# Recurrence chunks of a hybrid decoder layer: right-hand side's products before the inverse's first ones, GpSimd's first mask in two halves, bonus and decays behind the first additions

## The chip, the core and the metric

The kernel runs on one core of one Trainium2 chip. The metric is the device time of one execution in microseconds. Five engines work side by side and meet only through semaphores: TensorE (PE, with its weight loads shown apart as PEld), VectorE (DVE), ScalarE (ACT), GpSimd (POOL) and SyncE (SP), which issues DMAs.

## The reference, cut to what matters

One decoder layer over 1024 tokens of width 1024: an RWKV-7 recurrence of 8 heads x 64 beside differential attention, then cross-attention, then a top-4-of-32 expert network. The change touches the recurrence alone, which is

```python
def step(state, inp):
    r_t, w_t, k_t, v_t, kk_t, a_t = inp
    sa = jnp.einsum('bhvk,bhk->bhv', state, -kk_t)
    state = (state * w_t[:, :, None, :]
             + sa[..., None] * (kk_t * a_t)[:, :, None, :]
             + v_t[..., None] * k_t[:, :, None, :])
    return state, jnp.einsum('bhvk,bhk->bhv', state, r_t)
_, y = lax.scan(step, state0, scan_in)
```

with a bonus, `sum(r * k * r_k) * v` for each head, added to the result later. Everything is float32.

## The kernel before, in words

The recurrence (`rwkv_chunks`) is run in 8 chunks of 128 tokens. Within a chunk the step-by-step update is turned into products of 128x128 matrices for each of the 8 heads: the correlations of the tokens of the chunk (`corr`, four matrices for each head, masked by `corr_mask`), a triangular system whose inverse is wanted (`inv`, and transposed `invT`), a right-hand side (`rhs`), the solution, the new state and the output. The state couples one chunk to the next.

Each engine has its own list of instructions in the order in which the code of its block writes them, and each step adds one to the engine's semaphore; other engines wait for the value of a named step. So the order of the work is written out by hand. What one chunk does:

- **Start.** TensorE transposes `vc`, `kc` and `bc` into PSUM (L1134, step "turn"; ScalarE copies them to `vkb`, L1011) and makes the head sums for the bonus in `crossed` (L1136). VectorE makes `ar` (L1071, L1072) and scales the state (L1075).
- **Correlations and masks.** For each head TensorE writes 128x512 values into one of two PSUM banks (L1144, L1145), and VectorE multiplies them with the mask into `corr` (L1078). Two banks mean that TensorE is at most two heads ahead.
- **Level 0.** GpSimd multiplies the first matrix of every head with a level's mask into `part` (L989), 128x1024 values in one instruction. `part` has a single buffer. TensorE turns it over by a product with the identity into `straight` (L1152, two groups of four heads), VectorE adds the identity to `part` and to `straight` for `invT` and `inv` (L1095, L1097).
- **Right-hand side.** TensorE multiplies the state (L1158) and the correlations with the values (L1161) into `mixed`; ScalarE copies it to `rhs` (L1013), which is used only after the last level.
- **Levels 1 to 6** double the blocks of the inverse. In each, TensorE multiplies `part` with `inv` into `pairs` (L1170), ScalarE copies that (L1017), TensorE makes two further products (L1179, L1183), VectorE adds them into `inv` and `invT` (L1105, L1107), and GpSimd makes the next level's `part` (L989) meanwhile.
- **End.** TensorE solves (L1190), makes the new state and the output (L1196 to L1214); VectorE and ScalarE fold these in (L1114, L1118, L1022, L1025).

Beside this chain VectorE multiplies the bonus (L1082) and prepares the next chunk in parts: `prepare(i + 1, 0)` are the decays' differences (L1045, L1047, L1048, L1049), for which ScalarE takes exponentials after level 1's copies (L1001 to L1004); the further parts follow levels 1 to 3. GpSimd also copies `vc` once a chunk (L980).

One matmul of this float32 program stands as two records of the trace: the 8 products of L1152 are 16 records.

## Time and profile before

| | us |
|---|---|
| median of 3 runs | 3436.45 (3435.72 to 3442.59) |
| the profiled execution's own time | 3427.17 |
| its span | 3425.5 |
| busy in the span: PE, DVE, ACT, POOL | 2913.8, 1148.8, 669.2, 500.8 |
| mean granted TensorE clock | 0.922 |

The granted clock is TensorE's, as a share of full speed: 1.00 is 2.4 GHz and 0.50 is 1.2 GHz. The recurrence's 8 chunks lie between some 657 and 1130 us of the span, one after the other about every 60 us. The experts' products, from about 1760 us on, are the larger part of the kernel and are not touched.

### The profile page before, as it was taken

The numbers are of one execution on the slowest core, as the hardware profiler recorded it, in microseconds if no ns is written. First come the engines' busy times: TensorE is split into PE (matmuls) and PEld (weight loads), VectorE is DVE, ScalarE is ACT, GpSimd is POOL, SyncE is SP. The second block draws the span as 40 slices with busy tenths as digits, with TensorE's granted clock in tenths as the row PEclk, the third lists the DMA queues.
The fourth block names the chain that finished last, engine by engine and source line by source line (L and its number), as shares of the span: only waits on it lengthen the run. The fifth ranks groups of instructions, "written<-read, shape, count | busy, mean of one in ns | idle before, by whom it ended". The sixth has DMA issues, their size and how long they took to land. (4 is left out here: it accounts for less than half of the span.)

```text
span 3425.5 us, 54810 instructions
## 1 busy us (share of the span) xinstructions
PE 2913.8 (85%) x20974; PEld 2739.6 (80%) x20975; DVE 1148.8 (34%) x2439; ACT 669.2 (20%) x1261; POOL 500.8 (15%) x577
## 2 busy tenths in 40 slices
PE   7899888398999397986359999999999999999990
PEld 6876774288888396886359999999999999999990
DVE  2128221744443432232312222223222322232227
ACT  3139213111211312222001111111111111111111
POOL 0000001122213000001141110111111111111103
PEclk9999998699999698998579999999999999999995
DMA  6100210000000112014148877788888888888777
GB/s 223 32 25 1 56 43 7 0 1 0 0 0 0 51 55 69 12 56 151 53 135 298 286 269 270 270 292 294 291 292 293 288 297 286 292 294 276 270 260 260
DMA packets 320781, 543.61 MB, mean 159 GB/s; under 512 B 23584, under 2 KB 102176, under 8 KB 320672
## 3 DMA queue, kind: packets, MB, share of 16 engines
q1 hardware_dynamic: 301344, 499.67, 42.4%
q0 software_dynamic: 19360, 42.87, 4.1%
q8 instruction: 54, 0.88, 0.1%
q14 instruction: 23, 0.19, 0.0%
HBM read 506.01 MB, written 36.47 MB: 158 GB/s over the span
## 5 line engine op out<-in xcount | busy, mean ns | idle before, releaser
L2124 PE MATMUL experts_up<-experts_xs,g_pieces 128*128 128x144 f32 (+1 forms) x8192 | 1034.3, 290 | 114.4 <-DVE experts_xs L2053 77.4
L2124 PEld LDWEIGHTS experts_up<-experts_xs,g_pieces 128*128 128x128 f32 x8192 | 1027.7, 197 | 121.2 <-issue 121.2
L2147 PE MATMUL experts_down<-experts_hs,g_across 128*128 128x144 f32 (+1 forms) x3072 | 389.2, 289 | 0.0
L2147 PEld LDWEIGHTS experts_down<-experts_hs,g_across 128*128 128x128 f32 x3072 | 386.1, 190 | 0.0
L2002 POOL DMA_INDIRECT experts_x<-h_rows,experts_index x198 | 192.3, 971 | 1133.5 <-DVE experts_xs L2053 1078.6
L2083 DVE TENSOR_SCALAR experts_glu<-experts_up,experts_bias 128x176 f32<-128x176 f32 x256 | 102.3, 400 | 710.1 <-PE experts_up L2124 710.1
L2033 ACT ACTIVATE experts_sig<-experts_glu 128x352 f32<-128x352 f32 x128 | 63.7, 497 | 998.4 <-DVE experts_lin L2085 998.4
L2040 ACT ACTIVATE experts_yT<-experts_down,experts_bias 128x176 f32<-128x176 f32 x256 | 104.2, 407 | 381.1 <-PE experts_down L2147 305.8
L989 POOL TENSOR_TENSOR chunk_part<-chunk_corr,rwkv_level_mask 128x1024 f32<-128x1024 f32 x56 | 119.2, 2128 | 351.9 <-DVE chunk_corr L1078 188.5
L2074 DVE COPY experts_bias<-g_bias 128x24 f32 x32 | 5.8, 181 | 391.7 <-ACT experts_yT L2040 391.6
L2136 PE MATMUL experts_down<-experts_hs,g_across 128*128 128x144 f32 (+1 forms) x1024 | 133.3, 289 | 0.0
L2136 PEld LDWEIGHTS experts_down<-experts_hs,g_across 128*128 128x128 f32 x1024 | 130.1, 190 | 0.0
L1183 PE MATMUL chunk_crossed<-chunk_invT,chunk_corr 128*128 128x64 f32 x768 | 100.4, 275 | 0.0
L2085 DVE TENSOR_SCALAR experts_lin<-experts_up,experts_bias 128x176 f32<-128x176 f32 x256 | 100.4, 392 | 0.0
L1170 PE MATMUL chunk_pairs<-chunk_inv,chunk_part 128*128 128x128 f32 x768 | 96.4, 279 | 1.4 <-POOL chunk_part L989 1.4
L1183 PEld LDWEIGHTS chunk_crossed<-chunk_invT,chunk_corr 128*128 128x128 f32 x768 | 92.8, 192 | 0.3
L1170 PEld LDWEIGHTS chunk_pairs<-chunk_inv,chunk_part 128*128 128x128 f32 x768 | 89.6, 192 | 2.0 <-issue 1.8
L1017 ACT COPY chunk_corr<-chunk_pairs 128x512 f32<-128x512 f32 x96 | 56.2, 585 | 168.0 <-PE chunk_pairs L1170 168.0
L1105 DVE TENSOR_TENSOR chunk_inv<-chunk_inv,chunk_straight 128x256 f32<-128x256 f32 x80 | 33.7, 422 | 163.7 <-PE chunk_crossed L1183 163.7
L1481 PE MATMUL w_out_product<-w_out_w_high,hc_high 128*128 128x256 f32 x256 | 73.9, 289 | 16.2 <-DVE w_out_w_low L1413 16.2
L1179 PE MATMUL chunk_straight<-chunk_corr,chunk_invT 128*128 128x64 f32 x640 | 86.1, 277 | 0.0
L2053 DVE STREAM_TRANSPOSE experts_xs<-experts_x 128x256 f32<-128x256 f32 x198 | 68.3, 408 | 52.2 <-DMA experts_x<-h_rows,experts_index 52.2
(377 smaller groups left out, 4408.1 us busy)
## 6 DMA issues: line engine op xcount, KB each, us to landing
g_pieces<-in_w_dram SPq DMA_DIRECT2D x132, 2048.0 KB, 8.1
g_across<-in_w_dram SPq DMA_DIRECT2D x64, 2048.0 KB, 9.3
y_rows<-experts_y SPq DMA_DIRECT2D x132, 192.0 KB, 3.9
g_across<-in_w_ckv_dram SPq DMA_DIRECT2D x8, 1024.0 KB, 10.2
rkv_raw<-in_w_in_dram SPq DMA_DIRECT2D x13, 512.0 KB, 3.9
diff_qk_raw<-in_w_in_dram SPq DMA_DIRECT2D x9, 512.0 KB, 4.0
cross_q_raw<-in_w_cq_dram SPq DMA_DIRECT2D x9, 512.0 KB, 4.3
m_u<-in_x_dram SPq DMA_DIRECT2D x8, 512.0 KB, 10.1
```

Of the source, the lines that this page charges most:

```text
L989: pool.tensor_tensor(part[:], corr[:, :, 0, :], level_mask[:, l, :].unsqueeze(1).to_broadcast([P, H, P]), ALU.mult).then_inc(*pool_steps.s ...
L1170: ins = pe.matmul(pairs[:, g, j * P:(j + 1) * P], part[:, h, :], inv[:, h, :], start=(j == 0), stop=(j == 3), skip_group_check=True)
L1179: pe.matmul(level(straight, g, l)[:, j], invT[:, h, :], half(prod[:, h:h + 1, :], l, 0)[:, 0], start=(j == 0), stop=(j == 3), skip_group_c ...
L1183: ins = pe.matmul(level(crossed, g, l)[:, j], prod[:, h, :], half(invT[:, h:h + 1, :], l, 1)[:, 0], start=(j == 0), stop=(j == 3), skip_gr ...
L1481: pe.matmul(to, high[:, k, now], w_high[:, c % 2, k, :], start=(k == 0), stop=False)
L2002: pool.indirect_dma_start(x[:, g, :], None, quarters, bass.IndirectOffsetOnAxis(ap=index[:, 1, g:g + 1], axis=0)).then_inc(x_in, 16)
L2040: act.activation(yT[:, n, 0:N], down[:, n % 4, 0:N], ACT.Identity, bias=bias[:, 16 + n:17 + n]).then_inc(*act_y.step(f"d{n}"))
L2083: dve.tensor_scalar(glu[:, s, j, :], up[:, u % 4, 0:N], bias[:, 2 * u:2 * u + 1], LIMIT, ALU.add, ALU.min).then_inc(*dve_hidden.step(f"glu ...
L2085: dve.tensor_scalar(lin[:, s, j, :], up[:, u % 4, N:2 * N], bias[:, 2 * u + 1:2 * u + 2], 1.0 - LIMIT, ALU.add, ALU.max).then_inc(*dve_hid ...
L2124: ins = pe.matmul(up[:, u % 4, l * N:l * N + w], raw[c][:, k, at:at + 255:2], xs[:, k, 0:w], start=(k == 0), stop=(k == 7), skip_group_che ...
L2136: ins = pe.matmul(down[:, n, 0:w], raw[4][:, k, n * P:(n + 1) * P], hs[:, k, 0:w], start=(k == 0), stop=(k == 7), skip_group_check=True)
L2147: ins = pe.matmul(down[:, n % 4, 0:w], raw[4 + n // 4][:, k, (n % 4) * P:(n % 4 + 1) * P], hs[:, k, 0:w], start=(k == 0), stop=(k == 7), s ...
```

## The change

Four things, all in `rwkv_chunks`:

1. TensorE makes the right-hand side's products directly behind the correlations, after a new wait for the last head's mask, and the level-0 products after them. Before, level 0 came first.
2. GpSimd makes level 0's `part` in two instructions of four heads each. The first needs only the first four heads' masks, and TensorE waits for each half by itself.
3. VectorE does the four additions of level 0 directly behind the masks, and the bonus and `prepare(i + 1, 0)` behind them.
4. TensorE waits for the bonus before level 1's second products, since those write the PSUM bank from which the bonus is read.

The names of the steps are put in the new order. No arithmetic is added; GpSimd has one instruction more in each chunk.

```diff
--- before.py
+++ after.py
@@ -932,12 +932,12 @@
         groups = range(2)
         level_names = [f"l{l}_{what}{g}" for l in range(1, LEVELS) for what in ("p", "q") for g in groups]
         pe_steps = S.steps("products", ["turn", "bonus"] + [f"corr{h}" for h in range(H)] +
-                           ["l0_0", "l0_1", "rhs"] + level_names + ["solve", "state", "y"])
+                           ["rhs", "l0_0", "l0_1"] + level_names + ["solve", "state", "y"])
         act_steps = S.steps("act", ["v", "k", "b", "rhs"] +
                             [f"l{l}_p{g}" for l in range(1, LEVELS) for g in groups] + ["solve", "y"])
-        pool_steps = S.steps("pool", ["v"] + [f"part{l}" for l in range(LEVELS)])
-        dve_steps = S.steps("vector", ["r", "a", "edge", "state_in"] + [f"mask{h}" for h in range(H)] + ["bonus"] +
-                            [f"l0_{w}{g}" for g in groups for w in ("t", "s")] +
+        pool_steps = S.steps("pool", ["v", "part0_0", "part0_1"] + [f"part{l}" for l in range(1, LEVELS)])
+        dve_steps = S.steps("vector", ["r", "a", "edge", "state_in"] + [f"mask{h}" for h in range(H)] +
+                            [f"l0_{w}{g}" for g in groups for w in ("t", "s")] + ["bonus"] +
                             [f"l{l}_{w}{g}" for l in range(1, LEVELS) for g in groups for w in ("s", "t")
                              if not (l == LEVELS - 1 and w == "s")] +
                             ["add0", "add1", "scale0", "scale1"])
@@ -978,13 +978,16 @@
                     pool.wait_ge(pe_steps.sem, pe_steps.value("turn", i - 1))
                     pool.wait_ge(pool_steps.sem, pool_steps.so_far(i))
                     pool.tensor_copy(vc[:], u[:, 8:12, now]).then_inc(*pool_steps.step("v"))
-                    pool.wait_ge(dve_steps.sem, dve_steps.value(f"mask{H - 1}", i))
-                    for l in range(LEVELS):
-                        if l >= 1:
-
-                            pool.wait_ge(pe_steps.sem, pe_steps.value("l0_1" if l == 1 else f"l{l - 1}_p1", i))
-                            if l == 1:
-                                pool.wait_ge(dve_steps.sem, dve_steps.value("l0_s1", i))
+                    for g in groups:
+                        pool.wait_ge(dve_steps.sem, dve_steps.value(f"mask{4 * g + 3}", i))
+                        pool.tensor_tensor(
+                            part[:, 4 * g:4 * g + 4], corr[:, 4 * g:4 * g + 4, 0, :],
+                            level_mask[:, 0, :].unsqueeze(1).to_broadcast([P, 4, P]), ALU.mult).then_inc(*pool_steps.step(f"part0_{g}"))
+                    for l in range(1, LEVELS):
+
+                        pool.wait_ge(pe_steps.sem, pe_steps.value("l0_1" if l == 1 else f"l{l - 1}_p1", i))
+                        if l == 1:
+                            pool.wait_ge(dve_steps.sem, dve_steps.value("l0_s1", i))
                         pool.wait_ge(pool_steps.sem, pool_steps.so_far(i))
                         pool.tensor_tensor(
                             part[:], corr[:, :, 0, :],
@@ -1077,24 +1080,24 @@
                         dve.wait_ge(pe_steps.sem, pe_steps.value(f"corr{h}", i))
                         dve.tensor_tensor(corr[:, h], pairs[:, h % 2, :].rearrange("p (c n) -> p c n", n=P),
                                           corr_mask[:], ALU.mult).then_inc(*dve_steps.step(f"mask{h}"))
+                    eye = C.ident[:].unsqueeze(1).to_broadcast([P, 4, P])
+
+                    def four(x, g):
+                        return x[:, g * 4:g * 4 + 4, :]
+
+                    def bank(x, g):
+                        return x[:, g, :].rearrange("p (h n) -> p h n", n=P)
+                    for g in groups:
+                        dve.wait_ge(pool_steps.sem, pool_steps.value(f"part0_{g}", i))
+                        dve.tensor_tensor(four(invT, g), four(part[:], g), eye, ALU.add).then_inc(*dve_steps.step(f"l0_t{g}"))
+                        dve.wait_ge(pe_steps.sem, pe_steps.value(f"l0_{g}", i))
+                        dve.tensor_tensor(four(inv, g), bank(straight, g), eye, ALU.add).then_inc(*dve_steps.step(f"l0_s{g}"))
                     dve.wait_ge(pe_steps.sem, pe_steps.value("bonus", i))
 
                     dve.tensor_tensor(r, crossed[:, 1, :].rearrange("p (c n) -> p c n", n=P), vc[:],
                                       ALU.mult).then_inc(*dve_steps.step("bonus"))
                     if more:
                         prepare(i + 1, 0)
-                    eye = C.ident[:].unsqueeze(1).to_broadcast([P, 4, P])
-
-                    def four(x, g):
-                        return x[:, g * 4:g * 4 + 4, :]
-
-                    def bank(x, g):
-                        return x[:, g, :].rearrange("p (h n) -> p h n", n=P)
-                    dve.wait_ge(pool_steps.sem, pool_steps.value("part0", i))
-                    for g in groups:
-                        dve.tensor_tensor(four(invT, g), four(part[:], g), eye, ALU.add).then_inc(*dve_steps.step(f"l0_t{g}"))
-                        dve.wait_ge(pe_steps.sem, pe_steps.value(f"l0_{g}", i))
-                        dve.tensor_tensor(four(inv, g), bank(straight, g), eye, ALU.add).then_inc(*dve_steps.step(f"l0_s{g}"))
                     for l in range(1, LEVELS):
                         for g in groups:
                             dve.wait_ge(pe_steps.sem, pe_steps.value(f"l{l}_q{g}", i))
@@ -1146,13 +1149,7 @@
                                   skip_group_check=True).then_inc(*pe_steps.step(f"corr{h}"))
 
                     pe.wait_ge(act_steps.sem, act_steps.value("b", i))
-                    pe.wait_ge(pool_steps.sem, pool_steps.value("part0", i))
-                    for g in groups:
-                        for j in range(4):
-                            ins = pe.matmul(straight[:, g, j * P:(j + 1) * P], part[:, g * 4 + j, :], C.ident[:],
-                                            start=(j == 0), stop=(j == 3), skip_group_check=True)
-                        ins.then_inc(*pe_steps.step(f"l0_{g}"))
-
+                    pe.wait_ge(dve_steps.sem, dve_steps.value(f"mask{H - 1}", i))
                     pe.wait_ge(act_steps.sem, act_steps.value("y", i - 1))
                     for c in range(CT):
                         pe.matmul(mixed[:, 0, c * P:(c + 1) * P], ar[:, c, 0, :], state[:, c, :], start=(c == 0),
@@ -1161,6 +1158,13 @@
                         ins = pe.matmul(mixed[:, 0, h * 64:(h + 1) * 64], corr[:, h, 2, :], vkb[:, 0, h * 64:(h + 1) * 64],
                                         start=False, stop=(h == H - 1), skip_group_check=True)
                     ins.then_inc(*pe_steps.step("rhs"))
+                    for g in groups:
+                        pe.wait_ge(pool_steps.sem, pool_steps.value(f"part0_{g}", i))
+                        for j in range(4):
+                            ins = pe.matmul(straight[:, g, j * P:(j + 1) * P], part[:, g * 4 + j, :], C.ident[:],
+                                            start=(j == 0), stop=(j == 3), skip_group_check=True)
+                        ins.then_inc(*pe_steps.step(f"l0_{g}"))
+
                     for l in range(1, LEVELS):
                         pe.wait_ge(pool_steps.sem, pool_steps.value(f"part{l}", i))
                         for g in groups:
@@ -1170,6 +1174,8 @@
                                 ins = pe.matmul(pairs[:, g, j * P:(j + 1) * P], part[:, h, :], inv[:, h, :],
                                                 start=(j == 0), stop=(j == 3), skip_group_check=True)
                             ins.then_inc(*pe_steps.step(f"l{l}_p{g}"))
+                        if l == 1:
+                            pe.wait_ge(dve_steps.sem, dve_steps.value("bonus", i))
                         for g in groups:
                             pe.wait_ge(act_steps.sem, act_steps.value(f"l{l}_p{g}", i))
                             pe.wait_ge(dve_steps.sem, dve_steps.value(f"l{l - 1}_t{g}", i))
```

TensorE in a chunk, between the last head's correlations and level 1, before (a row is an instruction or a run of equal ones: what is written, what is read, and x the count; REGISTER_ALU and ISA rows only prepare waits):

```order
L1145 MATMUL chunk_pairs<-chunk_ar,chunk_kc 128x256
L1148 ISA
L1149 REGISTER_ALU
L1152 MATMUL chunk_straight<-g_ident,chunk_part 128x128 x8
L1156 ISA
L1158 MATMUL chunk_mixed<-chunk_state,chunk_ar 128x128 x4
L1161 MATMUL chunk_mixed<-chunk_vkb,chunk_corr 128x64 x8
L1165 REGISTER_ALU
L1167 REGISTER_ALU
L1170 MATMUL chunk_pairs<-chunk_inv,chunk_part 128x128 x4
L1167 REGISTER_ALU
L1170 MATMUL chunk_pairs<-chunk_inv,chunk_part 128x128 x4
```

And in the changed kernel, the same stretch:

```order
L1148 MATMUL chunk_pairs<-chunk_ar,chunk_kc 128x256
L1151 ISA
L1152 REGISTER_ALU
L1153 ISA
L1155 MATMUL chunk_mixed<-chunk_state,chunk_ar 128x128 x4
L1158 MATMUL chunk_mixed<-chunk_vkb,chunk_corr 128x64 x8
L1162 REGISTER_ALU
L1164 MATMUL chunk_straight<-g_ident,chunk_part 128x128 x4
L1162 REGISTER_ALU
L1164 MATMUL chunk_straight<-g_ident,chunk_part 128x128 x4
L1169 REGISTER_ALU
L1171 REGISTER_ALU
L1174 MATMUL chunk_pairs<-chunk_inv,chunk_part 128x128 x4
```

The products for `mixed` have moved ahead of those for `straight`, and each group of four heads has its own wait.

VectorE in a chunk from the last mask to the first additions of level 0, before:

```order
L1082 TENSOR_TENSOR m_u<-chunk_crossed,chunk_vc 128x4x128
L1044 ISA
L1045 ISA
L1045 TENSOR_TENSOR chunk_early<-rwkv_fall 128x512
L1046 REGISTER_ALU
L1047 REGISTER_ALU
L1047 TENSOR_TENSOR chunk_early<-chunk_early,rwkv_sig 128x512
L1048 COPY chunk_next_edge<-chunk_early 128x4
L1049 COPY chunk_next_edge<-rwkv_fall 128x4
L1093 ISA
L1095 TENSOR_TENSOR chunk_invT<-chunk_part,g_ident 128x512
L1096 REGISTER_ALU
```

And in the changed kernel from the last mask on:

```order
L1091 ISA
L1092 TENSOR_TENSOR chunk_invT<-chunk_part,g_ident 128x512
L1093 REGISTER_ALU
L1094 TENSOR_TENSOR chunk_inv<-chunk_straight,g_ident 128x512
L1091 REGISTER_ALU
L1092 TENSOR_TENSOR chunk_invT<-chunk_part,g_ident 128x512
L1093 REGISTER_ALU
L1094 TENSOR_TENSOR chunk_inv<-chunk_straight,g_ident 128x512
L1095 REGISTER_ALU
L1097 TENSOR_TENSOR m_u<-chunk_crossed,chunk_vc 128x4x128
L1047 ISA
L1048 ISA
```

The bonus (`m_u<-chunk_crossed,chunk_vc`) and the decays' differences (`chunk_early`, `chunk_next_edge`), which stood between the masks and the additions, now follow the additions.

## Rows read from the trace of the kernel before

**Rows 1.** The page, part 2: granted TensorE clock, tenths of full speed, 40 slices.
```profile
PEclk9999998699999698998579999999999999999995
```

**Rows 2.** Who waited for whom, 658 to 1128 us: us in total, times, longest.
```profile
POOL chunk_part L989 <- DVE chunk_corr L1078: 188.5, 8, 23.9
...
PE chunk_straight L1152 <- POOL chunk_part L989: 24.5, 8, 3.1
```

**Rows 3.** Timeline of one chunk, masks to level 1: start us, us, engine, line.
```profile
726.30 0.59 PE L1145 MATMUL chunk_pairs<-chunk_ar,chunk_kc 64*128 64x256 f32 x2
726.33 1.29 DVE L1078 TENSOR_TENSOR chunk_corr<-chunk_pairs,rwkv_corr_mask 128x512 f32<-128x512 f32 x2 [0.62 <-PE chunk_pairs L1145]
...
727.78 2.12 POOL L989 TENSOR_TENSOR chunk_part<-chunk_corr,rwkv_level_mask 128x1024 f32<-128x1024 f32 x1 [23.86 <-DVE chunk_corr L1078]
728.14 2.31 DVE L1045 TENSOR_TENSOR chunk_early<-rwkv_fall 128x512 f32 x1
...
729.96 3.63 PE L1152 MATMUL chunk_straight<-g_ident,chunk_part 128*128 128x128 f32 x16 [3.06 <-POOL chunk_part L989]
...
732.07 0.69 DVE L1097 TENSOR_TENSOR chunk_inv<-chunk_straight,g_ident 128x512 f32<-128x512 f32 x1
732.67 0.68 DVE L1095 TENSOR_TENSOR chunk_invT<-chunk_part,g_ident 128x512 f32<-128x512 f32 x1
...
733.42 1.06 PE L1158 MATMUL chunk_mixed<-chunk_state,chunk_ar 128*128 128x128 f32 x8
733.62 0.69 DVE L1097 TENSOR_TENSOR chunk_inv<-chunk_straight,g_ident 128x512 f32<-128x512 f32 x1 [0.27 <-PE chunk_straight L1152]
...
734.31 1.90 PE L1161 MATMUL chunk_mixed<-chunk_vkb,chunk_corr 128*128 128x64 f32 x16
734.47 2.12 POOL L989 TENSOR_TENSOR chunk_part<-chunk_corr,rwkv_level_mask 128x1024 f32<-128x1024 f32 x1 [4.57 <-DVE chunk_inv L1097]
...
736.72 2.05 PE L1170 MATMUL chunk_pairs<-chunk_inv,chunk_part 128*128 128x128 f32 x16 [0.51 <-POOL chunk_part L989]
...
738.63 1.10 PE L1179 MATMUL chunk_straight<-chunk_corr,chunk_invT 128*128 128x64 f32 x8
```

**Rows 4.** PE in two other chunks: the one quickest and the one slowest there.
```profile
846.14 0.59 PE L1145 MATMUL chunk_pairs<-chunk_ar,chunk_kc 64*128 64x256 f32 x2
849.80 3.45 PE L1152 MATMUL chunk_straight<-g_ident,chunk_part 128*128 128x128 f32 x16 [3.06 <-POOL chunk_part L989]
...
856.39 2.05 PE L1170 MATMUL chunk_pairs<-chunk_inv,chunk_part 128*128 128x128 f32 x16 [0.51 <-POOL chunk_part L989]
...
965.81 0.59 PE L1145 MATMUL chunk_pairs<-chunk_ar,chunk_kc 64*128 64x256 f32 x2
969.47 3.78 PE L1152 MATMUL chunk_straight<-g_ident,chunk_part 128*128 128x128 f32 x16 [3.06 <-POOL chunk_part L989]
973.04 1.92 PE L1158 MATMUL chunk_mixed<-chunk_state,chunk_ar 128*128 128x128 f32 x8
974.75 2.33 PE L1161 MATMUL chunk_mixed<-chunk_vkb,chunk_corr 128*128 128x64 f32 x16
976.91 2.00 PE L1170 MATMUL chunk_pairs<-chunk_inv,chunk_part 128*128 128x128 f32 x16
```

**Rows 5.** Stretches, PE alone: us, busy and records, granted clock, DMA.
```profile
661.60:665.00 3.40, 3.40 (x12) 0.50 0.00 0
...
671.80:675.20 3.40, 3.40 (x18) 0.50 0.00 0
...
726.90:729.90 3.00, 0.00 (x0) 1.00 0.00 0
729.90:733.30 3.40, 3.35 (x15) 0.50 0.00 0
...
736.70:767.20 30.50, 30.48 (x267) 1.00 0.00 0
...
968.80:975.60 6.80, 6.13 (x29) 0.50 0.00 0
```

## The prediction

> **What bounds the kernel now.** I read the page's line of granted clocks first [rows 1]: a slice is 85.6 us, the recurrence begins in the eighth, which reads 6, and fills the next five, which read 9, so the clock varies there and has to be looked at closer. The list of waits in that stretch [rows 2] shows one thing that TensorE waits for in all 8 chunks: GpSimd's first `part`, 24.5 us in 8 times, 3.1 at the longest. GpSimd in turn waits for the last mask, but that is idle time of an engine with little to do.
>
> The timeline of one chunk [rows 3] gives the chain around it. The last mask ends at 726.33 + 1.29 = 727.62. GpSimd starts at 727.78 and takes 2.12. TensorE, idle since it ended the correlations, starts level 0 (L1152) at 729.96; the row says that it was idle for 3.06. VectorE's last addition starts at 733.62, within 0.03 of the modelled end of L1152, and ends at 734.31. GpSimd starts level 1's `part` at 734.47 (one buffer, so not earlier), takes 2.12 again, and L1170 starts at 736.72. The right-hand side's products (733.42 to 736.21) run in the shadow of that second `part`. From L1170 on TensorE bounds the chunk: in 30.5 us of levels it is busy for 30.48 [rows 5], so whatever comes earlier or slower there moves the end one for one.
>
> The stretches [rows 5] show what the idle 3.06 us bring with them. The clock is 1.00 up to 729.9 and 0.50 in the 3.4 us behind, which is 1.2 instead of 2.4 GHz. L1152's 16 records take 3.63 us, where 16 records of the same 128x128 form take 2.05 in L1170 at full clock [rows 3]. In two other chunks L1152 takes 3.45 and 3.78, and in the second the half clock reaches over L1158 (1.92 instead of 1.06) and L1161 (2.33 instead of 1.90) [rows 4]. So every chunk has one long idle of TensorE, one fall of the clock with it, and pays for it on the products behind.
>
> From the start of the last L1145 row to L1170 the chunks of rows 3 and 4 take 10.42, 10.25 and 11.10 us. 10.25 and 11.10 are the least and the most of the seven chunks that follow the first one; their mean, read in the same way, is 10.58.
>
> **The changed chain.** All at full clock, on the times of rows 3:
> - Right-hand side first: it starts behind the last mask, at 727.62 + 0.06 (what L1152 needs after GpSimd: 727.78 + 2.12 to 729.96) = 727.68. It takes 736.21 - 733.42 = 2.79. It ends at 730.47.
> - GpSimd's halves: no row has this instruction on 512 values a partition. It takes at least half of 2.12, or 1.06, and at most the whole 2.12. The second half starts at 727.78 and ends at 728.84 to 729.90; the first is done during the masks. Either value is before 730.47, so the price is nothing. I take 1.1.
> - Level 0: 16 records need 738.63 - 736.72 = 1.91 as L1170 shows. First group issued by 731.43, second by 732.38; the ends are 0.14 later (2.05 - 1.91).
> - Additions: the first (`part` plus identity) is made during the right-hand side. It meets GpSimd's second half, and a row shows what that can do: L1045, 2.31 us under GpSimd's instruction, where VectorE's neighbours of the same size take 0.69. Even with all of 1.6 more it ends by 730, before it is needed. Then three more, 0.60 apart (732.07 to 732.67): 731.60, 732.20, 732.80, and 0.69 for the last: 733.49.
> - GpSimd: 0.16 later, 2.12 long: 735.77. TensorE 0.13 behind it (736.59 to 736.72): 735.90.
>
> From 726.30 that is 9.60 instead of 10.58: **0.98 us less in a chunk, 7.8 us in eight**.
>
> What moved behind the additions is covered. The bonus (0.69) starts at 733.40 and ends near 734.1, before TensorE begins level 1, so its new wait costs nothing. The decays' differences take 2.31 for L1045, 0.69 for another of the usual size and two copies of 8 values or less, to about 737.3. ScalarE wants them when it has copied level 1's first products, which are not made before 735.90 + 2.05 = 737.95; VectorE's next additions follow the second products, which start 1.91 behind L1170 and take 1.10 for the first part, so after 738.9. The cover is 0.6 us at least; if it were gone, ScalarE's exponentials would be late by the rest, and their reader comes a level later. ScalarE's copy `rhs` comes earlier and is used at the end of the chunk. No DMA or queue is touched.
>
> **Where the clock goes.** The change does not take away the idle time, it moves it. TensorE's idle before level 0 shrinks from 3.06 to about 0.8 (726.9 to 727.68). But nothing is left to do behind level 0: from 732.52 to 735.90, for 3.38 us, TensorE waits for the additions and the second `part`. In all 8 chunks an idle of 3.06 to 3.08 was followed by a half clock at once. A longer one should be too, and the products that then pay are level 1's, with no cover behind them. I price that from the same rows: what L1152, L1158 and L1161 took beyond 2.05, 1.06 and 1.90. In rows 3 this is 1.58, in rows 4 it is 1.40 and 1.73 + 0.86 + 0.43 = 3.02, and over the seven chunks the mean is 2.15. So the sum is -0.98 + 2.15 = +1.17 us a chunk, **+9.4 us in eight**. With 1.40 and 3.02 for it, the two ends are +3.4 and +16.3.
>
> The old chain also paid this, but part of it in the shadow of GpSimd: in rows 3 L1158 and L1161 could have been slower by 0.5 at no cost.
>
> The Trainium skill has a rule that speaks against this change, in "TensorE: Matmul & The Clock Gate", section "HAM oscillation — how this bites in real kernels": a burst of products behind a long wait starts with a throttled clock, every time anew, and costs half of the throttled time. Applied to half-clock stretches of 3.4 and 6.8 us, the page's half would be 1.7 and 3.4 a chunk, an estimate of +6 to +19 us in eight. This trace agrees on the mechanism: 1.58 lost in a stretch of 3.4.
>
> **The rivals.**
> - **The clock holds, 0.13.** If TensorE's work in front (4.7 us without a pause, where before there were correlations with pauses) keeps the granted clock at 1.00 across the idle 3.38 and over L1170, only the gain is left: -7.8 us. It decides at one place, the clock over the first L1170 of each chunk. Against it stand 8 falls in 8 chunks after 3.06 us.
> - **A mixed case, 0.25.** The fall comes in some chunks, or comes early and lies mostly in the idle time, so that a chunk loses 0.4 to 1.4. In the chunk of rows 4 at 965.81 the clock was already at half from 968.8, and 0.7 us of that stretch were idle. Sum: 8 x (-0.98 + 0.4 to 1.4), -4.6 to +3.4. That the change's reordering does nothing to the time belongs here.
> - **The half clock lasts, 0.14.** At the first chunk it held from 661.6 to 675.2, 13.6 us, although TensorE was busy for all 3.4 us of its first and of its last part [rows 5]: being busy is not enough to get the clock back. Two thirds of a level's records are 128x64 products, narrower than L1152's. If the clock stays at half for 10 us of levels, a chunk loses 5: +4.0 a chunk. In half of the chunks, the others as forecast, +21 us; in all of them +32.
> - **The half clock comes under the right-hand side, 0.05.** The idle before it is short, but the correlations have pauses too. Its 24 records at L1152's 3.63 / 16 = 0.227 take 5.4 instead of 2.8, and level 0 would take 3.6 instead of 1.9: +4.3 on the path, +26 us in eight with the gain.
>
> **How the numbers follow.** The forecast has the rest, 0.43. On the profiled execution it is 3427.17 + 9.4 = 3436.6. That execution is 9.3 below the median of the three runs; the difference is carried over unchanged: 3436.45 + 9.4 = 3445.8. The forecast's own range is 3439.9 to 3452.8. The range that should hold 8 in 10 takes in most of the mixed case below and the partly long half clock above: 3431 to 3458. A difference of 0.2%, 6.9 us, is about what a measurement of this kernel can tell from none. Faster by more: the clock holds, 0.13. Slower by more: three quarters of the forecast, 0.32, with the two last rivals, 0.19: 0.51. Within it: 0.36.
>
> **What would show it.** Right: L1174 (now level 1's first product) starts about 9.6 us after the last L1148 row instead of 10.6; TensorE's long idle stands before it, 3.4 us, released by GpSimd, and that before level 0 is gone; level 0 takes 1.9 to 2.1 us; the granted clock is 0.50 behind the idle, and one or two levels of each chunk take 7 us or more instead of 48 records x 30.48 / 267 = 5.48. GpSimd's halves take 1.1 us. Wrong: a clock of 1.00 over level 1 in most chunks, or a half clock under the right-hand side, or level 1's copies or second products that wait for VectorE.

## The result

| | us |
|---|---|
| before, median of 4 runs | 3436.52 (3435.72 to 3442.59) |
| changed, median of 4 runs | 3456.39 (3453.54 to 3458.44) |
| ratio of changed to before, with 95% interval | 1.0053 (1.0036 to 1.0071) |
| profiled execution before | 3427.17, span 3425.5 |
| profiled execution of the changed kernel | 3455.29, span 3453.7 |

The changed kernel is slower by 19.9 us. The forecast was +9.4, with a range of 3431 to 3458: the sign and the range held, and the forecast was half of what came.

### The profile page after: what moved, and what is told of

It is laid out like the page before. It is cut to its first block and busy times, and to the rows that moved or that the text cites. A ratio compares the mean times of both kernels' runs of the same rounds, so it can differ in the third digit from the quotient of the medians.

```text
span 3453.7 us, 54838 instructions
## 1 busy us (share of the span) xinstructions
PE 2934.1 (85%) x20974; PEld 2751.9 (80%) x20975; DVE 1148.7 (33%) x2439; ACT 664.6 (19%) x1261; POOL 505.4 (15%) x585
## 5 line engine op out<-in xcount | busy, mean ns | idle before, releaser
L1174 PE MATMUL chunk_pairs<-chunk_inv,chunk_part 128*128 128x128 f32 x768 | 106.5, 297 | 26.5 <-POOL chunk_part L992 26.5
L992 POOL TENSOR_TENSOR chunk_part<-chunk_corr,rwkv_level_mask 128x1024 f32<-128x1024 f32 x48 | 102.2, 2129 | 182.7 <-PE chunk_pairs L1174 136.9
L1174 PEld LDWEIGHTS chunk_pairs<-chunk_inv,chunk_part 128*128 128x128 f32 x768 | 99.1, 209 | 28.0 <-issue 24.5
L1487 PE MATMUL w_co_product<-w_co_w_high,w_co_high 128*128 128x256 f32 x256 | 73.9, 289 | 13.4 <-DVE w_co_w_low L1419 13.4
## 6 DMA issues: line engine op xcount, KB each, us to landing
g_across<-in_w_ckv_dram SPq DMA_DIRECT2D x8, 1024.0 KB, 10.1
m_u<-in_x_dram SPq DMA_DIRECT2D x8, 512.0 KB, 10.3
```

Of the source, the lines that this page charges most:

```text
L992: pool.tensor_tensor(part[:], corr[:, :, 0, :], level_mask[:, l, :].unsqueeze(1).to_broadcast([P, H, P]), ALU.mult).then_inc(*pool_steps.s ...
L1174: ins = pe.matmul(pairs[:, g, j * P:(j + 1) * P], part[:, h, :], inv[:, h, :], start=(j == 0), stop=(j == 3), skip_group_check=True)
L1487: pe.matmul(to, high[:, k, now], w_high[:, c % 2, k, :], start=(k == 0), stop=False)
```

## The profile after

First the changed kernel's line of granted clocks (the page, part 2), which answers to [rows 1]. The recurrence now lies at 655 to 1144 us.

```profile
PEclk9999998798998698998579999999999999999995
```

The eighth slice reads 7 instead of 6, but the tenth and the thirteenth read 8 instead of 9. Inside the recurrence something costs clock that did not before. The list of waits of the same stretch, 655 to 1130 us (us in all, times, longest), answers to [rows 2]:

```profile
POOL chunk_part L983 <- DVE chunk_corr L1081: 181.0, 16, 20.0
...
POOL chunk_part L992 <- DVE chunk_inv L1094: 45.9, 8, 7.9
...
PE chunk_pairs L1174 <- POOL chunk_part L992: 26.5, 8, 3.4
```

TensorE's wait of 24.5 us in 8 times before level 0 has become one of 26.5 us in 8 times before level 1. It has moved, and it is longer. The timeline of a quiet chunk, one whose clock falls only at level 1 (start, us, engine, line), for [rows 3]:

```profile
722.16 0.59 PE L1148 MATMUL chunk_pairs<-chunk_ar,chunk_kc 64*128 64x256 f32 x2
723.63 1.15 PE L1155 MATMUL chunk_mixed<-chunk_state,chunk_ar 128*128 128x128 f32 x8 [0.88 <-DVE chunk_corr L1081]
724.62 1.90 PE L1158 MATMUL chunk_mixed<-chunk_vkb,chunk_corr 128*128 128x64 f32 x16
726.35 2.00 PE L1164 MATMUL chunk_straight<-g_ident,chunk_part 128*128 128x128 f32 x16
731.80 3.14 PE L1174 MATMUL chunk_pairs<-chunk_inv,chunk_part 128*128 128x128 f32 x16 [3.44 <-POOL chunk_part L992]
734.73 1.59 PE L1185 MATMUL chunk_straight<-chunk_corr,chunk_invT 128*128 128x64 f32 x8
736.16 1.05 PE L1189 MATMUL chunk_crossed<-chunk_invT,chunk_corr 128*128 128x64 f32 x8
```

From the last correlation row to level 1 it is 731.80 - 722.16 = 9.64 us, where the prediction had 9.60. Level 0 takes 2.00, at full clock. TensorE then sits idle for 3.44 us, and level 1's first products take 3.14 instead of 2.05. The same stretch on the other engines, in the first chunk:

```profile
661.77 1.29 DVE L1081 TENSOR_TENSOR chunk_corr<-chunk_pairs,rwkv_corr_mask 128x512 f32<-128x512 f32 x2 [0.62 <-PE chunk_pairs L1148]
662.98 0.68 DVE L1092 TENSOR_TENSOR chunk_invT<-chunk_part,g_ident 128x512 f32<-128x512 f32 x1
663.14 1.53 POOL L983 TENSOR_TENSOR chunk_part<-chunk_corr,rwkv_level_mask 128x512 f32<-128x512 f32 x1 [2.67 <-DVE chunk_corr L1081]
...
668.28 0.68 DVE L1094 TENSOR_TENSOR chunk_inv<-chunk_straight,g_ident 128x512 f32<-128x512 f32 x1
668.88 0.68 DVE L1097 TENSOR_TENSOR m_u<-chunk_crossed,chunk_vc 128x512 f32 x1
669.13 2.12 POOL L992 TENSOR_TENSOR chunk_part<-chunk_corr,rwkv_level_mask 128x1024 f32<-128x1024 f32 x1 [4.45 <-DVE chunk_inv L1094]
...
671.38 3.53 PE L1174 MATMUL chunk_pairs<-chunk_inv,chunk_part 128*128 128x128 f32 x16 [3.44 <-POOL chunk_part L992]
```

The order of events is the one worked out: last addition, second `part`, level 1. Nothing waits for the bonus, which is done 1.8 us before level 1 starts.

So the quiet chunk explains little of 20 us. The third chunk shows where the rest is (TensorE only):

```profile
783.40 0.63 PE L1148 MATMUL chunk_pairs<-chunk_ar,chunk_kc 64*128 64x256 f32 x1
783.73 0.63 PE L1147 MATMUL chunk_pairs<-chunk_ar,chunk_bc 64*128 64x256 f32 x1
784.16 1.05 PE L1148 MATMUL chunk_pairs<-chunk_ar,chunk_kc 64*128 64x256 f32 x2
786.09 2.07 PE L1155 MATMUL chunk_mixed<-chunk_state,chunk_ar 128*128 128x128 f32 x8 [0.88 <-DVE chunk_corr L1081]
787.96 3.51 PE L1158 MATMUL chunk_mixed<-chunk_vkb,chunk_corr 128*128 128x64 f32 x16
791.26 3.30 PE L1164 MATMUL chunk_straight<-g_ident,chunk_part 128*128 128x128 f32 x16
797.70 3.51 PE L1174 MATMUL chunk_pairs<-chunk_inv,chunk_part 128*128 128x128 f32 x16 [3.14 <-POOL chunk_part L992]
```

The right-hand side takes 5.38 us instead of 2.89 and level 0 3.30 instead of 2.00, and the whole of the correlations takes 9.35 instead of 7.46. Two stretches of the same chunk (us, busy and records, granted clock, DMA):

```profile
780.40:794.00 13.60, 12.72 (x51) 0.50 0.00 0
797.40:800.80 3.40, 3.10 (x14) 0.50 0.00 0
```

The clock was at half from within the correlations to within level 0, 13.6 us, and fell once more behind the idle. Read out for every chunk from the two timelines, in us. The length runs from the first record of the `kc` correlations (L1145, now L1148) to that of the next chunk. "To level 1" starts at the last such record alone, not at the row of two that the timelines show, and so is 0.2 less. Level 1 runs to level 2's first product.

| chunk | 1 | 2 | 3 | 4 | 5 | 6 | 7 | 8 |
|---|---|---|---|---|---|---|---|---|
| length, before | 62.3 | 59.8 | 60.0 | 59.7 | 60.0 | 60.5 | 59.6 | |
| length, changed | 60.4 | 60.6 | 65.7 | 60.6 | 65.7 | 60.6 | 65.6 | |
| to level 1, before | 10.8 | 10.2 | 10.4 | 10.0 | 10.4 | 10.9 | 10.1 | 10.6 |
| to level 1, changed | 9.4 | 9.4 | 13.1 | 9.4 | 13.1 | 9.4 | 13.1 | 9.3 |
| level 1, before | 5.5 | 5.5 | 5.5 | 5.5 | 5.5 | 5.5 | 5.5 | 5.4 |
| level 1, changed | 6.9 | 7.0 | 6.9 | 7.0 | 6.9 | 7.0 | 6.9 | 7.0 |

From that first record to the start of the last chunk's solution the recurrence grew from 470.4 to 488.0 us, by 17.6. The spans of the two profiled executions differ by 28.2 us in all. Of the rest 12.9 lie behind the recurrence, in code that the change does not touch, and -2.3 before it. That part varied in the runs below too, though no edit touches it (2295 to 2306 us in them, 2297 and 2310 in these two). The changed kernel's second profile (e10) has 2295 there. So it isn't explained by the change.

The first chunk was 2.4 us longer before than its next ones, and this isn't the change's doing either. TensorE, nearly idle, was at half clock ahead of the recurrence, in code that no edit touches, and in this execution the half clock reached 1.5 us into the chunk's correlations:

```profile
607.00:658.20 51.20, 6.00 (x22) 0.50 0.00 0
```

In the changed kernel that stretch ended at 654.0 us, ahead of the chunk. It reached into the first chunk also in e11, e3 and e8 below, with old and new code, and in none of the others.

## The experiments

Two theories. **Clock:** the change's added time is TensorE's half clock, behind the moved idle and in three chunks' correlations; GpSimd's halves and VectorE's new order are harmless or good. **Waits:** it is VectorE's late bonus and decays, and TensorE's new wait for them. Ratios are against the kernel before, run on the same chip, with 95% intervals; the recurrence is measured as above, on one profiled execution each. For e2 and e3 that was the slowest of their runs (3461.63 and 3439.95 us), for e4 and e8 the fastest (3429.04 and 3420.48), so these rows don't show a typical execution.

| run | median us | before there | ratio | recurrence us |
|---|---|---|---|---|
| level 0 first (e1) | 3410.34 | 3430.49 | 0.994 (0.9923 to 0.9957) | 450.6 |
| right-hand side first, alone (e2) | 3453.50 | 3430.49 | 1.0063 (1.0046 to 1.0079) | 494.5 |
| changed, idle filled (e3) | 3433.33 | 3430.49 | 1.0005 (0.9996 to 1.0015) | 480.9 |
| before, idle filled (e4) | 3433.71 | 3430.49 | 1.0011 (1.0001 to 1.002) | 474.2 |
| changed, correlations filled (e5) | 3454.34 | 3429.78 | 1.0064 (1.004 to 1.0088) | 495.5 |
| changed, both filled (e6) | 3426.48 | 3429.78 | 0.999 (0.998 to 1.0) | 461.3 |
| level 0 first, correlations filled (e7) | 3399.98 | 3429.78 | 0.9916 (0.99 to 0.9933) | 442.5 |
| halves alone (e8) | 3424.49 | 3429.78 | 0.9986 (0.9975 to 0.9996) | 467.3 |
| VectorE's order alone (e9) | 3427.63 | 3428.88 | 0.9995 (0.9983 to 1.0007) | 467.0 |

**e1: level 0 first again, the rest of the change kept.**

```diff
-                    pe.wait_ge(dve_steps.sem, dve_steps.value(f"mask{H - 1}", i))
+                    for g in groups:
+                        pe.wait_ge(pool_steps.sem, pool_steps.value(f"part0_{g}", i))
+                        for j in range(4):
+                            ins = pe.matmul(straight[:, g, j * P:(j + 1) * P], part[:, g * 4 + j, :], C.ident[:],
+                                            start=(j == 0), stop=(j == 3), skip_group_check=True)
+                        ins.then_inc(*pe_steps.step(f"l0_{g}"))
```

The same lines go away behind the right-hand side, and the names of the steps are put in the old order.

> The changed kernel with one part undone: TensorE makes level 0's products before the right-hand side's again, and GpSimd's two halves and VectorE's new order stay. Clock theory (the added time is the half clock, which TensorE's idle between level 0 and level 1 and the phase of the chunks bring; halves and new order are harmless or good): the right-hand side again lies under the second part of GpSimd, level 0 starts at once with the first half, no idle of 3 us is left, and from the last correlation row to level 1 it is about 7.0 us instead of 10.6 before and 9.4 changed. That is 3.6 us a chunk or 25 to 30 us in eight below the kernel before, with the clock at 1.00 in most levels. Wait theory (the added time is the later bonus and decays on VectorE and TensorE's new wait for the bonus): level 1 stays at 6.9 us or more in this kernel too, and it is 5 to 20 us slower than before.

It is 20 us faster than before: 0.6% below, where the changed kernel is 0.5% above. Undoing this one part turns the sign. The waits theory falls. In the timeline of a chunk:

```profile
723.86 0.59 PE L1148 MATMUL chunk_pairs<-chunk_ar,chunk_kc 64*128 64x256 f32 x2
...
724.38 1.16 PE L1155 MATMUL chunk_straight<-g_ident,chunk_part 128*128 128x128 f32 x8
...
726.84 1.16 PE L1155 MATMUL chunk_straight<-g_ident,chunk_part 128*128 128x128 f32 x8 [1.30 <-POOL chunk_part L983]
...
727.84 1.06 PE L1161 MATMUL chunk_mixed<-chunk_state,chunk_ar 128*128 128x128 f32 x8
...
731.15 2.05 PE L1173 MATMUL chunk_pairs<-chunk_inv,chunk_part 128*128 128x128 f32 x16 [0.52 <-POOL chunk_part L992]
```

The first group starts without an idle, the second behind one of 1.30, and the right-hand side fills the wait for the second `part`. From the correlation row to level 1 it is 7.29 us; 7.0 had been expected. The miss against 25 to 30 us is the clock again: the fifth and the seventh chunk had a half clock in their correlations and took 59.4 us instead of 56.7, and the first 60.0.

**e2: TensorE's order alone, on the kernel before.**

```diff
-                    pe.wait_ge(pool_steps.sem, pool_steps.value("part0", i))
-                    for g in groups:
...
+                    pe.wait_ge(dve_steps.sem, dve_steps.value(f"mask{H - 1}", i))
                     pe.wait_ge(act_steps.sem, act_steps.value("y", i - 1))
...
                     ins.then_inc(*pe_steps.step("rhs"))
+                    pe.wait_ge(pool_steps.sem, pool_steps.value("part0", i))
+                    for g in groups:
...
```

The wait for GpSimd and level 0's products move behind the right-hand side.

> The kernel before with TensorE's order alone changed (right-hand side first, behind a wait for the last mask); one GpSimd instruction for level 0 and VectorE's old order. Clock theory: as the changed kernel within 5 us, so +13 to +25 us against before: the second idle of 3.4 us and the half clock behind it are there, and the halves never mattered for it, since the right-hand side's products cover the whole instruction of GpSimd. Wait theory: within 5 us of the kernel before, or faster by up to 8 us.

As the clock theory had it, +0.63% where the changed kernel has +0.53%. The reordering on TensorE alone brings a loss of that size. Level 0 starts 3.98 us behind the last correlation record with GpSimd's single instruction as with the halves: under the right-hand side's cover the halves were worth nothing. The falls aren't the same ones, though. The clock fell in the correlations of the fourth and the seventh chunk and under the right-hand side of the second, and in the first and the last it stayed at half for 10 us or more over level 1, which took 10.3 and 9.3 us there.

**e3: the changed kernel with the idle filled.** 12 products behind level 0 go to a PSUM bank that nobody reads at that time; they add work to the kernel and no result.

```diff
+                    for _ in range(12):
+                        pe.matmul(mixed[:, 1, 0:P], C.ident[:], ar[:, 0, 1, :], start=True, stop=True, skip_group_check=True)
```

> The changed kernel with 12 products added behind level 0 whose result nobody reads, 24 records or 2.7 us at full clock, where TensorE else sits idle for 3.4 us. Clock theory: they keep the granted clock at 1.00 over level 1, which then takes 5.5 us instead of 6.9 to 7.0, a gain of 1.45 us a chunk or 12 us in eight; whether the three chunks with a half clock in their correlations keep it depends on where the chunks come to lie, so 12 to 28 us below the changed kernel. Wait theory: level 1 is as long as in the changed kernel, and the time the same or longer.

Level 1 takes 5.5 us in all eight chunks. So the half clock in level 1 does come from the idle before it. The median is 20 us below e2's on the same chip, that of the kernel before and not under it. In the profiled execution, the slowest of ten, the half clock still came in the correlations or the right-hand side of five chunks (60.7 to 64.6 us, and the last one), while the three undisturbed ones took 58.9 to 59.1.

**e4: the kernel before with its own idle filled**, by the same 12 products behind the correlations. TensorE's wait for ScalarE's last copy of `mixed`, whose bank they write, moves ahead of them; level 0 starts 3.45 us behind the last correlation record in the undisturbed chunks as before, so that wait costs nothing there.

> The kernel before with the same 12 products added behind the correlations, where TensorE is idle for 3.06 us. Clock theory: level 0 runs at full clock, 1.9 to 2.1 us instead of 3.45 to 3.79, and the stretch from the last correlation row to level 1 falls from 10.6 to about 9.0 us: 10 to 15 us faster than before. Wait theory has nothing against this, but if the time stays as it is, the half clock had never cost anything and my price for it in the changed kernel falls too.

The 10 to 15 us did not come: the kernel was 3.2 us slower. Level 0 does run at full clock,

```profile
843.34 2.94 PE L1151 MATMUL chunk_mixed<-chunk_ar,g_ident 128*128 128x128 f32 x24
846.48 2.05 PE L1155 MATMUL chunk_straight<-g_ident,chunk_part 128*128 128x128 f32 x16 [0.20 <-POOL chunk_part L989]
848.37 1.06 PE L1161 MATMUL chunk_mixed<-chunk_state,chunk_ar 128*128 128x128 f32 x8
849.26 1.90 PE L1164 MATMUL chunk_mixed<-chunk_vkb,chunk_corr 128*128 128x64 f32 x16
852.76 2.46 PE L1173 MATMUL chunk_pairs<-chunk_inv,chunk_part 128*128 128x128 f32 x12 [1.59 <-POOL chunk_part L989]
```

and the way to level 1 is 9.7 us instead of 10.4. But the right-hand side is done early now, 1.59 us of idle stand before level 1, and the clock falls elsewhere: in two chunks level 1 took 7.0, in four the correlations (from their first `kc` record to the last) took 8.0 to 8.2 instead of 6.55. A fall that is prevented in one place came in another. And where that happened, the added products ran at half clock too and held level 0 up, as in the sixth chunk:

```profile
967.33 5.49 PE L1151 MATMUL chunk_mixed<-chunk_ar,g_ident 128*128 128x128 f32 x24
972.61 2.02 PE L1155 MATMUL chunk_straight<-g_ident,chunk_part 128*128 128x128 f32 x16
```

Level 0 starts 5.84 us behind the last correlation record there instead of 3.45.

**e5: the changed kernel with the correlations' pauses filled**, by 2 products before the first correlation and 3 before the third.

```diff
+                    for _ in range(2):
+                        pe.matmul(mixed[:, 1, 0:P], C.ident[:], kc[:, 0, :], start=True, stop=True, skip_group_check=True)
                     pe.wait_ge(dve_steps.sem, dve_steps.value("state_in", i))
...
+                        if h == 2:
+                            for _ in range(3):
+                                pe.matmul(mixed[:, 1, 0:P], C.ident[:], kc[:, 0, :], start=True, stop=True, skip_group_check=True)
```

> The changed kernel with 5 products (10 records) added whose result nobody reads: 2 before the first correlation and 3 before the third, where TensorE is idle for 0.3 and 0.8 us. If the half clock in three chunks' correlations comes from these pauses in products of half height, it goes: all chunks take 60.6 us, the time falls by some 13 to 16 us against the changed kernel, and level 1 still takes 6.9 to 7.0 us. Rival: the fall there is a late effect of the one behind the long idle, or of when a chunk begins, and pauses don't matter; then some chunks still take about 65 us and the time stays within 5 us of the changed kernel.

The 13 to 16 us did not come, though what was filled was cured: every chunk's correlations took 6.57 us. The kernel was 24.6 us slower than before where the changed one is 19.9, and its recurrence was 7.5 us longer than the changed kernel's. In the fourth chunk (same columns as above):

```profile
842.10:848.90 6.80, 6.59 (x38) 1.00 0.00 0
848.90:852.20 3.30, 2.24 (x12) 1.00 0.00 0
852.20:859.10 6.90, 6.90 (x36) 0.51 0.00 0
859.10:862.50 3.40, 0.71 (x6) 1.00 0.00 0
862.50:866.00 3.50, 3.03 (x14) 0.51 0.00 0
```

The fall came later, behind the correlations' end with its idle of 0.88, and lay over the right-hand side and level 0; 3.4 us at full clock, mostly idle, followed, and then the next fall. This came in four chunks, and in three the half clock stayed over level 1 for 10.2 us or more, so that level 1 took 9.0 to 10.3 us. So the correlations' own pauses are a cause, but not the only one that has to go.

**e6: both fillings in the changed kernel.**

> The changed kernel with both kinds of added products, 5 among the correlations and 12 behind level 0. If all that the change added is the half clock, every chunk now takes about 59.1 us as the undisturbed ones of the run with 12 did, 0.9 less than before the change: 5 to 12 us faster than the kernel before, and 25 to 30 us faster than the changed one. Rival (something else in the change costs time): not faster than before.

Every chunk but the last takes 59.15 us. From 657 to 1090 us the clock holds:

```profile
657.00:1090.00 433.00, 413.18 (x3374) 1.00 0.00 0
```

The recurrence takes 461.3 us, 9.1 less than before (2.4 of them for the first chunk's slow start there) and 26.7 less than the changed kernel. In time it is 3.3 us faster than before, less than the 5 to 12 expected and with an interval that ends at 1.0; in the trace the recurrence's gain is plain. With the clock held the change's chain is worth what its first term said, and nothing else in it costs time. A timed pair with the changed kernel on one chip wasn't made; e5, on the same chip, was 27.9 us slower.

**e7: level 0 first, and the correlations filled.**

> The kernel with GpSimd's halves and VectorE's new order but level 0 first, with the 5 products among the correlations added. There two chunks of eight had a half clock in the correlations and took 2.7 us longer. If the pauses make it, all chunks take 56.7 us, or up to 0.3 more where the added products delay a correlation: 3 to 8 us faster than without them, 22 to 28 faster than the kernel before. Rival: no change within 3 us, or slower by what the added products take, 10 records or 1.1 us a chunk.

29.8 us faster than before, more than the 22 to 28 expected: 3399.98 against 3429.78, the best of this study. Every chunk takes 56.8 us, and again

```profile
657.00:1090.00 433.00, 411.74 (x3349) 1.00 0.00 0
```

The 10 added records cost 0.07 us a chunk against e1's quiet ones, and its two falls in the correlations are gone. The first chunk's is gone too; in e1 it came at 703.9 us, within the solution, and why it is absent here isn't shown.

**e8: GpSimd's halves alone** (VectorE's bonus and decays back before the additions, level 0 first).

> The kernel before with GpSimd's halves alone; VectorE does the bonus and the decays before the additions, as before. VectorE is then busy with them until 3.7 us after the last mask, so the additions end about when they did (0.5 us earlier), although level 0's products are made 2 to 3 us earlier. TensorE does the right-hand side early and then is idle for 3 us before level 1, with the half clock behind it: level 1 takes 6.5 to 7 us. Sum: -0.5 + 1.4 a chunk, 0 to +15 us against before. Rival: the halves carry the whole gain of the kernel with level 0 first, -15 to -25 us.

This missed both: it was 5.3 us faster, where 0 to 15 us slower had been expected and the rival had 15 to 25 faster. Level 1 starts 8.66 us behind the last correlation record instead of 10.4, so 1.7 earlier where 0.5 had been worked out. VectorE's first instruction for the decays is 1.0 of the difference: beside a GpSimd instruction of 1.16 us it took 1.27 instead of 2.31, and the additions began that much earlier.

```profile
725.48 1.16 POOL L982 TENSOR_TENSOR chunk_part<-chunk_corr,rwkv_level_mask 128x512 f32<-128x512 f32 x1 [2.67 <-DVE chunk_corr L1080]
725.91 1.27 DVE L1047 TENSOR_TENSOR chunk_early<-rwkv_fall 128x512 f32 x1
```

The half clock over level 1 came in four chunks only, though it lasted 10 us in two of them.

**e9: VectorE's new order alone.**

> The kernel before with VectorE's new order alone (additions, then bonus and decays, and TensorE's wait for the bonus); one GpSimd instruction for level 0 and level 0 first on TensorE. The additions wait for TensorE's level 0 in any case, which is at half clock behind the idle of 3.06 us, so the chunk's chain stays as it was: from the last correlation row to level 1 10.0 to 10.9 us, the sum within 5 us of the kernel before. That and the run with the halves alone would show that the gain of both together needs both. Wait theory, last form: the later bonus delays level 1's second products; then level 1 takes over 5.6 us at full clock and the time is 5 us or more above before.

As expected: 1.3 us faster, inside the noise; 10.0 to 10.6 us to level 1, and level 1 in 5.5. Halves and order are worth 3.3 us a chunk together on the way to level 1 (10.4 to 7.07) and 1.7 and 0.2 apart. Either one alone leaves the other engine last.

**The two kernels once more**, unaltered.

> The changed kernel once more, unaltered, for a second profile. If the falls in the correlations follow from when the chunks come and are steady, again 2 to 4 of the 8 chunks take about 65 us and the others 60.4 to 60.9; if they were chance, another count from 0 to 8.

> The kernel before once more, unaltered. If it keeps its clock in the correlations for a reason, again all chunks from the second on take 59.5 to 60.5 us; if that was luck in one execution, one or more take 62 us or longer.

Both repeat to 0.1 us in every chunk: the changed kernel has its 65.7 us in the third, fifth and seventh again and a recurrence of 488.0, the other 59.6 to 60.5 from the second on and 470.4. So the falls aren't the chance of one execution. One execution each took 3442.22 and 3426.13 us, 16.1 apart.

**Why three chunks and why these.** The traces of all the runs answer it. In each of the 13 profiled executions every change of the granted clock lies on one even raster of time, to 0.003 us. What counts is where a point of that raster lies in a chunk, measured from the chunk's first correlation record:

| chunks | raster point at 4.06 to 4.64 us | number | clock fell within the correlations |
|---|---|---|---|
| nothing added among the correlations | yes | 15 | in all 15, at that point |
| the same | no; the nearest at 4.03 and 4.78 | 61 | in none |
| products added there (e5, e6, e7) | yes | 6 | in none |
| the same | no | 18 | in none |

The four first chunks that began at half clock are left out. In all 76 chunks with nothing added, the correlation records of the first 4.06 us start at the same times behind the first, to 0.005 us. In the kernel before, no chunk from the second on has a raster point in that stretch; the seventh comes nearest, with 4.01. In the changed one the third, the fifth and the seventh have it at 4.43 to 4.46, in both profiles. There a long and a short chunk together, 126.3 us, are to 0.01 us a whole number of the raster's spacings, so every second chunk comes to lie at the same place. No run shifted the chunks and did nothing else; the rule rests on these 100 chunks as they came to lie.

## Why the prediction was right, and where its size failed

- **The chain, -0.98 us a chunk.** Right: 9.64 instead of 9.60 from correlation row to level 1, and 9.43 instead of a mean of 10.4 from the last record in quiet chunks, -0.94.
- **Prices set at nothing.** Right: the halves lie under the right-hand side, the bonus and the decays under level 1. e6 has all of them and is faster in the recurrence. The second half took 1.53 us, between the two bounds; 1.1 had been taken.
- **The moved idle and the half clock behind it.** The mechanism was right in 8 chunks of 8: an idle of 3.44 (3.38 worked out) and level 1 at half clock, which e3 takes away. Its size was too large: 2.15 was taken from the old chunks, 6.95 - 5.5 = 1.45 came. In the old chunks the half clock lasted 3.4 us in three, at a cost of 1.40 to 1.67, and 6.8 us in four, at 2.3 to 3.0; over the new level 1 it lasted 3.4 us in all eight.
- **What failed in the size** is the sentence that puts a half clock under the right-hand side at 0.05 as a rival, and with it a sum that lets every chunk lose only behind its idle. In three chunks the clock fell in the correlations, and 1.6 us there, 3.7 on the way to level 1 and -0.15 in level 1 came on top: 5.2 us a chunk, 15.5 in all. With 8 x (-0.94 + 1.45) = +4.1, and -2.4 for the first chunk, which is no effect of the change, this gives +17.2 of the 17.6 measured. The price worked out for that rival, 4.3 us a chunk, was near; its chance was far too small, and the correlations themselves were not in it. By the prediction's own list a half clock under the right-hand side was a sign of being wrong, and three chunks of eight showed it. That it came in three chunks is luck as far as the prediction goes: it hung on where the chunks came to lie on the raster, and nothing in the prediction placed them. So it is luck too that the time stayed inside the range. The rows had the warning: the first chunk ran its correlations at half clock with TensorE busy in all of 661.6 to 665.0 [rows 5].
- **The rule of the Trainium skill** ("TensorE: Matmul & The Clock Gate", "HAM oscillation — how this bites in real kernels") had the burst behind a long wait start throttled, which this trace bears out; its estimate of +6 to +19 us holds 17.6, but for another reason, since most of the loss lay in products with short pauses. For these the same page has a section, "A second HAM failure mode: psum-queue depth-cycling": small idles between groups of products can make the clock go up and down too. The trace agrees, with a fall at 780.4 us where the idles were 0.77 us or less; the prediction had not drawn on it.

What stays open is what sets the raster's place against the first chunk, and why the half clock, once there, lasts 3.4 us in one place and 13.6 in another. The first raster point in the first chunk lay at 1.5 us in the four executions whose early half clock reached into it (before, e11, e3, e8), and at 2.5 to 2.6 us in the others, or 2.1 with products added ahead; this doesn't go by the new code or the old.

## What to carry to other kernels

Moving work into an idle stretch of TensorE helps only if it isn't taken from the cover of another one: look for what fills the next wait once the step is gone. When the clock falls behind an idle, cost the new place of the idle by what stands behind it, and count every thin or broken stretch nearby as a place where the clock can fall too. A change can also lose time in code that it leaves alone, by moving it in time: here 15.5 of 17.6 us began in untouched correlations. A test with useless products in the gaps tells how much of a stage is clock, if all the gaps are filled; with one of two filled (e3, e4, e5) the clock still fell elsewhere. Where pauses are short such products can pay for themselves: here 10 records a chunk came with a recurrence 8.1 us shorter.

## What the runs showed of the hardware

- A long idle is not needed for the half clock. In the changed kernel's third chunk it fell at 780.4 us, within the correlations, where TensorE had no idle longer than 0.8 us. These products have 64 rows instead of 128 (`64*128` in the rows). Filling the pauses took the fall away there (e5, e6, e7).
- Every change of the granted clock lies on an even raster of time within an execution, to 0.003 us in each of 13, and whether the correlations' pauses cost the clock is decided by where they lie on it (with nothing added there the clock fell in 15 chunks of 15 with a raster point at 4.06 to 4.64 us, and in none of the 61 without).
- GpSimd's mask on 512 values a partition takes 1.15 to 1.54 us, not half of the 2.12 for 1024:

```profile
L983 POOL TENSOR_TENSOR chunk_part<-chunk_corr,rwkv_level_mask x16: 1151/1343/1536, 659.3 to 1102.3; 128x512 f32<-128x512 f32 x16
```

  The row above with 1.53 starts beside one of VectorE's additions of two SBUF operands. The 1.5 us are the second halves', which meet that addition; in e8, where they don't, the second half took 1.16.
- VectorE's subtraction for the decays takes 0.82 us in the first preparation, with GpSimd at rest, and 2.31 in each chunk, where it meets GpSimd's instruction of 2.12, before and after the change. Beside one of 1.16 it took 1.27 (e8). The changed kernel's, with minimum, median and greatest in ns:

```profile
L1048 DVE TENSOR_TENSOR chunk_early<-rwkv_fall x8: 818/2311/2314, 644.7 to 1048.4; 128x512 f32 x7, 128x512 f32<-128x512 f32 x1
```
